# Layer 1's rotation tables and lambda, moved from ahead of the last feed-forward product's weight splits to between its token tiles' norms

## What is computed

```python
def rope_tables(n):
    t = jnp.arange(n)
    pos = jnp.stack([t // GRID_W, t % GRID_W], -1).astype(jnp.float32)
    nq = HEAD_DIM // 4
    inv = ROPE_THETA ** (-jnp.arange(nq, dtype=jnp.float32) / nq)
    ang = pos[:, :, None] * inv
    return jnp.cos(ang), jnp.sin(ang)
...
    # layer 0, last step
    h = h + g2 * ffn(rms_norm(h, norm2_g[l]) * (1 + sc2) + sh2)
    hc = hc + modc[5] * ffn(rms_norm(hc, norm2_g[l]) * (1 + modc[4]) + modc[3])
...
    # layer 1, first steps
    a_lat = rms_norm(h, norm1_g[l]) * (1 + sc1) + sh1
    a_ctx = rms_norm(hc, norm1_g[l]) * (1 + modc[1]) + modc[0]
...
    lam = (jnp.exp(jnp.sum(lam_q1.astype(f32) * lam_k1.astype(f32)))
           - jnp.exp(jnp.sum(lam_q2.astype(f32) * lam_k2.astype(f32))) + lam_init)
    p_lat = h_lat @ w_in
    # queries and keys: rms_norm(., gain) and then apply_rope(., cos, sin)
```

## Time and profile before

| | us |
|---|---|
| median of 3 runs | 1921.24 (1919.27 to 1925.32) |
| the profiled execution | 1925.34 |
| its span, first to last instruction | 1923.5 |
| TensorE busy in it | 1751.9 (91%) |
| VectorE busy | 1250.8 (65%) |
| ScalarE busy | 824.2 (43%) |
| GpSimd busy | 134.6 (7%) |

### The profile page before, as it was taken

The page is one execution under the profiler, slowest core; times in us unless marked ns, Lnnn a source line. Parts: engine busy times, 40 slices in busy tenths (PEclk is TensorE's granted clock), DMA queues, the critical chain, the costliest instruction groups (busy, mean ns, idle before and its releaser), DMA issues. The chain is left out here.

```text
span 1923.5 us, 22047 instructions
## 1 busy us (share of the span) xinstructions
PE 1751.9 (91%) x8958; PEld 1466.7 (76%) x8958; DVE 1250.8 (65%) x1709; ACT 824.2 (43%) x999; POOL 134.6 (7%) x128
## 2 busy tenths in 40 slices
PE   4896999899999987899979999999969998889998
PEld 2774777788788866798768888888859766669986
DVE  5356686368755544675668888888886554566643
ACT  5322232422212213333356667776744434435532
POOL 1130000200110011320100000000120000000000
PEclk9896999999999998899869999999999989999999
DMA  7431332245655431211148898888854511144553
GB/s 294 112 110 66 132 132 89 86 175 218 237 212 180 149 137 66 88 45 56 63 162 300 320 336 328 316 321 317 323 202 159 200 60 39 66 149 171 190 187 126
DMA packets 61437, 332.59 MB, mean 173 GB/s; under 512 B 16836, under 2 KB 17411, under 8 KB 28178
## 3 DMA queue, kind: packets, MB, share of 16 engines
q1 hardware_dynamic: 56080, 321.54, 46.4%
q10 hardware_dynamic: 4354, 6.32, 1.0%
q0 software_dynamic: 896, 3.26, 0.5%
HBM read 329.96 MB, written 1.13 MB: 172 GB/s over the span
## 5 line engine op out<-in xcount | busy, mean ns | idle before, releaser
L1983 DVE TENSOR_TENSOR wlo__65<-raw__64,whi__66 128x2048 fp32r<-128x2048 f32 (+2 forms) x64 | 149.4, 2335 | 95.6 <-ACT whi__66 L1468 95.6
L1983 DVE TENSOR_TENSOR wlo__61<-raw__60,whi__62 128x2048 fp32r<-128x2048 f32 (+2 forms) x65 | 145.1, 2232 | 94.3 <-ACT whi__62 L1468 94.2
L1468 ACT ACTIVATE whi__62<-raw__60 128x2048 fp32r<-128x2048 f32 (+2 forms) x65 | 118.9, 1829 | 115.3 <-DMA raw__60<-in_ffn_w 62.7
L1468 ACT ACTIVATE whi__66<-raw__64 128x2048 fp32r<-128x2048 f32 (+2 forms) x64 | 120.7, 1886 | 102.7 <-DMA raw__64<-in_ffn_w 37.9
L1983 DVE TENSOR_TENSOR wlo__69<-raw__68,whi__70 128x2048 fp32r<-128x2048 f32 (+4 forms) x50 | 106.6, 2133 | 28.3 <-ACT whi__70 L1468 28.2
L2016 DVE SCALAR_TENSOR_TENSOR wsum__71<-raw__68,silu_rows 128x1024 f32<-128x1024 f32 x84 | 100.0, 1220 | 5.4 <-DMA raw__68<-in_ada_w 4.9
L1468 ACT ACTIVATE whi__70<-raw__68 128x2048 fp32r<-128x2048 f32 (+4 forms) x50 | 87.5, 1750 | 13.7 <-DMA raw__68<-in_w_ff 11.6
L2982 POOL TENSOR_TENSOR keep__58<-keep__58,keep__59 128x1 f32<-128x1 f32 (+3 forms) x48 | 49.2, 1027 | 630.9 <-DVE keep__58 L2055 630.9
L2238 DVE TENSOR_REDUCE keep__58<-ps 128x1 f32<-128x256 f32 (+1 forms) x104 | 56.6, 545 | 23.2 <-PE ps L892 16.4
L1983 DVE TENSOR_TENSOR wlo__229<-raw__228,whi__230 128x2048 fp32r<-128x2048 f32 (+1 forms) x24 | 50.7, 2111 | 11.7 <-ACT whi__230 L1468 11.7
L1983 DVE TENSOR_TENSOR wlo__225<-raw__224,whi__226 128x2048 fp32r<-128x2048 f32 (+1 forms) x24 | 52.8, 2200 | 0.0
(11 more groups left out here) (1084 smaller groups left out, 5469.4 us busy)
## 6 DMA issues: line engine op xcount, KB each, us to landing
raw__68<-in_ada_w SPq DMA_DIRECT2D x26, 1024.0 KB, 4.9
raw__64<-in_moe_w SPq DMA_DIRECT2D x24, 1024.0 KB, 6.5
raw__60<-in_moe_w SPq DMA_DIRECT2D x24, 1024.0 KB, 6.3
raw__68<-in_moe_w SPq DMA_DIRECT2D x16, 1024.0 KB, 5.6
raw__224<-in_moe_w SPq DMA_DIRECT2D x16, 1024.0 KB, 5.0
raw__228<-in_moe_w SPq DMA_DIRECT2D x16, 1024.0 KB, 6.1
raw__135<-in_ada_w SPq DMA_DIRECT2D x13, 1024.0 KB, 5.2
raw__64<-in_ffn_w SPq DMA_DIRECT2D x11, 1024.0 KB, 5.2
```

What stands on the lines that cost most here:

```text
L1468: e.activation(t.hi(), t.raw(), ACT.Copy).then_inc(*did("hi", i))
L1983: e.tensor_tensor(t.lo(), t.raw(), t.hi().bitcast(F32), ALU.subtract).then_inc(*did("lo", i))
```

## The change

`tables()` moves in the vector program from ahead of the product's loop over token tiles into it, behind the gate, the norm step and with them the splits of token tile 0. The Exp of lambda moves in the scalar program from ahead of `norm_by_token` to behind the scaling of token tile 1 in it. No instruction is added or taken away, and the transfers stay where they are.

```diff
@@ scalar program, norm_by_token
                 if t == 1:
                     norm_scale(N, 1)
+                    if N == "o":
+                        for s, n in due(("lam_s",)):
+                            e.wait_ge(s, n)
+                        e.activation(LM[:, 2:4], LM[:, 0:2], ACT.Exp).then_inc(*did("lam_e"))
@@ scalar program, ahead of norm_by_token("o", ...)
         e.dma_start(RW, I["moe_router"][0].rearrange("(k p) e -> p k e", p=128)).then_inc(*did("rw", by=16))
-        for s, n in due(("lam_s",)):
-            e.wait_ge(s, n)
-        e.activation(LM[:, 2:4], LM[:, 0:2], ACT.Exp).then_inc(*did("lam_e"))
         norm_by_token("o", ("ff2", 1))
@@ vector program, the feed-forward's loops
                 if blk and half:
                     for v in range(2):
                         gain("n1b", sc1b, v, 6, 7)
-                    tables()
                     at["ahead"] = 1
@@
                     if blk and half and t < 3:
                         norm_scale("o", t)
+                    if blk and half and t == 0:
+                        tables()
```

## The result

| | before | after |
|---|---|---|
| median, run beside each other (11 and 11 runs) | 1924.0 us | 1914.4 us |
| lowest and highest | 1919.27, 1925.96 | 1910.59, 1919.29 |
| the profiled execution's span | 1923.5 | 1915.4 |

The ratio is 0.9957, 95% interval 0.9946 to 0.9968: the change saves 8.3 us (6.2 to 10.4). The direction was forecast right and the size too large by 4.1 us, a third of the 12.4 forecast; the median lies within the range (1903.5 to 1915.0) but near its upper end. What the prediction had wrong are two terms of its sum, both too large: the wait that goes (9.7 us), since the tile landed later than assumed, and the clock, taken as kept (2.7 us). The miss of 5.5 us in the median has two halves: the kernel before ran 2.8 us slower beside it than the median that the forecast started from (1924.0 against 1921.24), and the two medians lie 9.6 us apart in place of 12.4.

What follows compares the result with a forecast made beforehand. TensorE was taken as held 11.3 us ahead of the third weight tile by the order of two queues. Saving 9.7 (wait) + 2.7 (clock), with 0 for backlog and tables, gave 12.4 us: median 1908.9 us, range 1903.5 to 1915.0.

Steps and rivals of the forecast that it cites:

- What bounds the place: TensorE's 11.3 us wait ahead of the product's third weight tile comes from the order of two queues, not data.
- (a): Ahead of the third weight tile, TensorE's wait shrinks as its split starts at landing: 9.7 us saved, 1.6 us stay.
- a slower landing: Sign of a wrong forecast: the third weight tile's first split starts well after 713.4; landing was taken as 6.1 us.
- (b): TensorE's clock stays full behind the third tile's shortened wait, so 13 matmuls run faster: 2.7 us, bounds 0 and 2.8.
- the clock falls in the short gap: Rival, chance 0.12: the 13 matmuls behind the third tile's wait stay slow, only 9.7 us gained, 1911.5 us.
- (c): Backlog on VectorE and ScalarE through the token tiles' norm ends 1.0 us before reaching the path: cost 0, at most 2 us.
- (d): Tables and Exp result are read only after both norms, VectorE's 4 us covered by TensorE's matmuls: no cost.
- Slot 2's high part: Rival, chance 0.06: TensorE waits for whi__70 ahead of the third tile, gap 4.8 us, gain 6.5 us, 1914.7 us.
- Given back: Rival, chance 0.07: a later wait takes up the gain, about 1920 us.
- Slower: Rival, chance 0.03: TensorE's clock stays at half through 109 matmuls up to the transposes, +10.9 us, 1932.1 us.

Runs made afterwards that it cites:

- e2: The kernel before with only the Exp moved, the tables left ahead of the splits: 1920.1 us, ratio 0.9990.
- e8b: The kernel before with the Exp moved and ScalarE's thirteen small transfers issued one product earlier, tables left ahead of the splits: 1914.8 us, ratio 0.9971.
- e11: The changed kernel with only the mask's and the two routing transfers issued one product earlier: 1902.9 us, one execution.
- e10: The changed kernel with only the ten short-row transfers issued one product earlier: 1906.0 us, one execution.
- e1: The changed kernel with all thirteen small ScalarE transfers issued one product earlier: 1908.6 us, ratio 0.9932 to the kernel before.
- e3: The changed kernel again, with no edit, for a second profile: 1910.2 us, ratio 0.9941 to the kernel before.
- e9b: e1 with layer 1's second weight tile also split ahead of token tile 3's square and scaling: 1903.4 us, ratio 0.9910 to the kernel before.
- e4b: The changed kernel with the 32 table products made three times over, 6.8 us more on VectorE: 1913.9 us, ratio 0.9971 to the kernel before.
- e5: The kernel before with the thirteen small ScalarE transfers issued one product earlier, tables and Exp unmoved: 1918.5 us, ratio 0.9976.

## Why the prediction was right or wrong

**What bounds the place: right.** TensorE was held by the order of two queues. e2 and e8b, which undo VectorE's half alone, have waits of 7.82 and 4.20 us, against 0.55 to 3.18 and 0.51 with it.

**(a) The wait, 9.7 us: mechanism right, size off by the landing.** The split took 3.42 us (3.41 taken). The landing of 6.1 us was read from one execution and was the shortest of seven with the ten short transfers in place (6.1, 7.0, 7.6, 6.5, 7.1, 6.2, and 7.0 in e11). In the profile after it was 7.6, so 1.6 us more of the wait stayed: 8.1 saved and not 9.7. The prediction named "a slower landing" as what would make it wrong, and that is what came. That ten small transfers of ScalarE cause it, the row could not say; e10 and e11 show it.

**(b) The clock, 2.7 us: the step that failed.** "So I take the clock as kept" rested on one gap of 2.2 us and on a clock that held for over 2 us after the stop, and took the upper end of a range. Neither row reaches to the 3.2 us of gap that came, and the first was luck: of the twelve profiles, which all have this gap of 2.0 to 2.2 us, four show a granted clock at half for 3.4 us behind it and eight don't. Behind the later gap it fell at 3.18 and 4.20 us, and not at 2.73. From the third tile's first matmul to the end of A it is 28.1 us where the clock holds (e1, e3, e9b, e10, e11), 29.7 in the profile after, and 30.7 before. So in the profile after (b) gave 1.1 in place of 2.7. The rule of the Trainium skill that was weighed there (TensorE: Matmul & The Clock Gate, Part 1: The HAM clock gate), that the same gap can fall well or badly from one execution to the next, is what these profiles show, with four drops in twelve behind the same gap: the bound of 0 to 2.7 was right, and the end taken was not. The rival "the clock falls in the short gap" is what the profiled execution did, at 3.2 us of gap, and with 3.4 us of slow clock and not 5.7.

**Sum of the trace.** 8.1 + 1.1 = 9.2 us, against 12.4: 1.6 short by the landing and 1.6 by the clock. The second pair of profiles has 10.8 (56.94 - 46.15). By the means of both pairs TensorE reaches its third tile 8.6 us earlier (9.7 forecast), and the rest of A is 1.4 us shorter (2.7 forecast).

**(c) The backlog: cost right, with more slack than forecast.** 4.8 us in the profile after and 2.4 in e3, in place of 1.0. In the profile after that is mostly TensorE's delay by landing and clock; in e3 slot 2's tile landed 0.2 us behind the restart of TensorE, and not 1.1 as in the sum. The Exp began 1.30 us after its table load did, as the earlier trace rows had it and not with a drain behind it, which is where the Trainium skill (ScalarE: Activation LUTs, What ACT_TABLE_LOAD costs) gets its 2.66. With 6.8 us more the path is reached (e4b), so the mechanism is real, and the change stayed short of it.

**(d) Tables and Exp at no cost: right.** No wait for them appears in the changed kernel.

**The other rivals.** Slot 2's high part: refuted. ScalarE's timeline of the changed kernel:

```profile
718.75 1.92 ACT L1468 ACTIVATE whi__70<-raw__68 128x2048 fp32r<-128x2048 f32 x1 [1.24 <-DMA raw__68<-in_od_w_in]
```

There, in e3 and in e11 TensorE starts before whi__70 is done (719.45 against 718.75 + 1.92 = 720.67), and within 0.2 us of the end of wlo__132. Given back: B keeps all of A's gain (10 us in both means). Slower: behind the gap the clock was back after 3.4 us in the change.

**The base.** Half of the median's miss is the three runs of the kernel before, which came out 2.8 us below its median of eleven.

## What to carry to other kernels

Where an engine's queue holds a small side job with a late input ahead of work that the critical engine waits for, move it behind that work on every engine that takes part: half of the move brought 1.9 us here by the traces, which the times can't tell from none, and the whole 8 to 11. Then price what is late next, a landing above all, from several executions or as a range, and look at what else is issued in the same microseconds: small transfers with short rows delayed a large one by 2 to 3.5 us. Don't count a clock kept or lost behind a gap of 2 to 3.3 us as certain either way.

## What the runs showed of the hardware that was not expected

- A weight transfer of 768 KB on SyncE's queue took 4.0 to 4.3 us to land, and 6.1 to 7.6 when ten transfers in short rows on ScalarE's queue fell into the same microseconds. The tile's bytes started late, with the DMA share at 0.10 to 0.15 meanwhile. The mask and the routing's transfers (256, 192 and 32 KB) had no such effect (4.2 us in e10).
- VectorE's instruction now and then takes longer than its like: two of the 32 table products 1.28 us in place of 0.18 in e5, and wlo__132 2.64, 2.62 and 2.50 us in e1, e9b and e10 in place of 1.76. In each of them a fetch of 8 KB on an instruction queue lies within the instruction or just ahead of it, but in e3 one lies within wlo__132 too, and it takes 1.76. So the fetch alone doesn't explain it, and the cause stays open. In e1, e9b and e10 it makes the split 0.7 to 0.9 us longer, and TensorE waits 0.5 us for it, where 0 to 0.3 was expected of e1.
- A gap of the same length and place on TensorE, 2.0 to 2.2 us, cost nothing in eight profiles and 3.4 us at half the clock in four. One of 3.3 us, ahead of layer 1's second weight tile, went with the half clock in eight of ten, for 3.4 us in four of them and 6.8 in the other four. Where the next wait was for data anyway (e3), even that cost vanished in it.
